# Every second pair of expert-up units by Strassen's seven block products, sums on GpSimd, all lowering on VectorE

## The reference, cut to what matters

```python
def peer(h, w_query, sub_keys1, sub_keys2, expert_down, expert_up):
    ...
    u = expert_down[ib]
    act = jax.nn.gelu(jnp.einsum("td,thkd->thk", hb, u), approximate=False)
    v = expert_up[ib]
    return jnp.einsum("thk,thkd->td", gb * act, v)
```

## Time and profile before

| | |
|---|---|
| median of 3 runs (lowest to highest) | 1389.7 us (1389.6 to 1393.01) |
| profiled execution, its own time | 1390.32 us |
| its span, first to last instruction | 1388.5 us |
| PE busy | 1362.2 us, 98% |
| DVE busy | 1037.2 us, 75% |
| ACT busy | 887.4 us, 64% |
| POOL busy | 653.5 us, 47% |

### The profile page before, as it was taken

The page is one execution under the profiler, slowest core; times in us unless marked ns, Lnnn a source line. Parts: engine busy times, 40 slices in busy tenths (PEclk is TensorE's granted clock), DMA queues, the critical chain, the costliest instruction groups (busy, mean ns, idle before and its releaser), DMA issues.

```text
span 1388.5 us, 32152 instructions
## 1 busy us (share of the span) xinstructions
PE 1362.2 (98%) x9840; PEld 1267.2 (91%) x9840; DVE 1037.2 (75%) x2233; ACT 887.4 (64%) x1861; POOL 653.5 (47%) x503
## 2 busy tenths in 40 slices
PE   7999999999999999999999999999999999999998
PEld 4798999999999989999999999999998888888886
DVE  6778867888988496439999868888876666666665
ACT  5668765555446665547888687777765555555554
POOL 4896783000006868688888887777730000000000
PEclk9999999999999999999999999999999999999998
DMA  9776565988983633565555554444455666566662
GB/s 343 272 253 228 198 244 189 323 320 317 336 331 122 215 127 123 188 216 168 182 182 183 182 168 154 159 156 151 154 166 194 195 192 189 194 196 193 189 194 90
DMA packets 79798, 283.84 MB, mean 204 GB/s; under 512 B 8822, under 2 KB 8950, under 8 KB 79611
## 3 DMA queue, kind: packets, MB, share of 16 engines
q1 hardware_dynamic: 79738, 283.07, 59.7%
HBM read 281.99 MB, written 1.05 MB: 204 GB/s over the span
## 4 chain that ended last, share of the span: by engine, by line
PE 79%; POOL 6%; issue 5%; PEld 3%; DVE 3%; ACT 2%; DMA 1%; PEldq 0%; POOLq 0%; SPq 0%; DVEq 0%
PE psA L1821 19%; PE psA L1825 19%; PE psA L1824 19%; POOL w_lo L563 6%; PE psD L1821 6%; PE psD L1824 5%; PE psD L1825 5%; PE psD L2283 1%; PEld psA L1821 1%; PE psD L2284 1%; PEld psA L1825 1%; PEld psA L1824 1%; DMA xT<-x 1%; DVE arena L1540 1%; PEld psD L2240 0%
## 5 line engine op out<-in xcount | busy, mean ns | idle before, releaser
L628 ACT CAST w_hi<-raw 128x512 fp32r<-128x512 f32 x864 | 529.5, 620 | 424.7 <-PE psA L1821 306.8
L563 POOL TENSOR_TENSOR w_lo<-raw,w_hi 128x512 fp32r<-128x512 f32 x476 | 632.7, 1348 | 353.6 <-ACT w_hi L628 343.1
L1821 PE MATMUL psA<-h_hi,w_hi 128*128 128x256 f32 x1568 | 452.8, 289 | 0.7 <-POOL w_lo L563 0.5
L1824 PE MATMUL psA<-h_lo,w_hi 128*128 128x256 f32 x1568 | 443.0, 283 | 0.0
L1825 PE MATMUL psA<-h_hi,w_lo 128*128 128x256 f32 x1568 | 442.9, 282 | 0.0
L1099 DVE TENSOR_TENSOR w_lo<-raw,w_hi 128x512 fp32r<-128x512 f32 x388 | 266.1, 691 | 152.7 <-ACT w_hi L628 151.6
L1821 PEld LDWEIGHTS psA<-h_hi,w_hi 128*128 128x128 f32 x1568 | 300.0, 191 | 4.3 <-issue 1.5
L1824 PEld LDWEIGHTS psA<-h_lo,w_hi 128*128 128x128 f32 x1568 | 300.2, 191 | 0.1
L1825 PEld LDWEIGHTS psA<-h_hi,w_lo 128*128 128x128 f32 x1568 | 299.9, 191 | 0.0
L1821 PE MATMUL psA<-w_hi,u_hi 128*128 128x512 f32 x512 | 199.4, 389 | 0.4 <-DVE u_lo L1162 0.4
L1825 PE MATMUL psA<-w_hi,u_lo 128*128 128x512 f32 x512 | 199.2, 389 | 0.0
(11 more groups left out here) (391 smaller groups left out, 2212.5 us busy)
## 6 DMA issues: line engine op xcount, KB each, us to landing
raw<-expert_down SPq DMA_DIRECT2D x128, 512.0 KB, 3.2
raw<-expert_up SPq DMA_DIRECT2D x128, 512.0 KB, 4.2
arena<-ada SPq DMA_DIRECT2D x96, 512.0 KB, 5.3
raw<-gateup SPq DMA_DIRECT2D x44, 512.0 KB, 5.4
raw<-feat SPq DMA_DIRECT2D x28, 512.0 KB, 3.8
raw<-win SPq DMA_DIRECT2D x24, 512.0 KB, 3.3
raw<-down SPq DMA_DIRECT2D x22, 512.0 KB, 6.1
raw<-wout SPq DMA_DIRECT2D x20, 512.0 KB, 3.2
```

Source lines behind the costliest of these rows:

```text
L563: nc.gpsimd.tensor_tensor(w_lo[:, s * HALF:(s + 1) * HALF], raw_half(n), w_hi[:, s * HALF:(s + 1) * HALF].bitcast(F32), ALU.subtract).then ...
L628: nc.scalar.copy(w_hi[:, n % SLOTS * HALF:(n % SLOTS + 1) * HALF], raw_half(n)).then_inc(hi_ready, 1)
L1821: first = mm(o, w[0], m[0], start=start, stop=False, skip_group_check=True)
L1824: mm(o, w[0], m[1], start=False, stop=False, skip_group_check=True)
```

## The change

The first 16 expert-up units and the last four stay as they were. The 108 between them become 27 groups of four: two units in the old way ("singles", 12 matmuls each) and one pair of units as a product of 2x2 blocks. Of a pair, U gives the blocks a11, a12, a21, a22 (unit by token block) and W gives b11, b12, b21, b22 (unit by half). Strassen's method, in Winograd's form, takes seven products instead of eight, 21 matmuls instead of 24, each of a block or a sum of blocks of U with a block or a sum of blocks of W (three blocks and four sums on either side):

- POOL makes four sums of 128x512 for W (`sum_weights`, into `w_sums`) and four of 128x128 for U (`sum_pairs`, one of them written over a21).
- ACT copies seven halves of W for a pair (three blocks, four sums), and the U blocks and sums as one 128x512 and one 128x384.
- DVE lowers all of them, as it did before: 11 halves in a group in place of eight, and the same two pieces of U.
- `w_hi` and `w_lo` get eight slots in place of four; every second pair from the fourth on is loaded into `raw_spare`.
- Four of the seven products add into the four banks of `psD`. After the last group ACT copies one bank, DVE adds the banks into `y_sums` (four adds), and the final copies of `psA` become adds of `psA` and `y_sums`, all on DVE.

The core of the diff:

```diff
+def up_lowered(g, i):
+    return UP_AT + GROUP_HALVES * g + i + 1
...
@@ SP
+            def load_singles(g):
+                for k in range(2):
+                    if g == 0:
+                        sp.wait_ge(lo_ready, UP_AT - 6 + 2 * k)
+                    else:
+                        single_free(g - 1, k)
...
@@ POOL
+            def sum_weights(g, k, in0, in1, op, read):
+                if g:
+                    pool.wait_ge(lo_ready, up_lowered(g - 1, read))
+                if k in (2, 3):
+                    pool.wait_ge(sem("w_sums"), 4 * g + (1, 3)[k - 2])
+                nc.gpsimd.tensor_tensor(w_sums[:, k, :], in0, in1, op).then_inc(sem("w_sums"), 1)
+            def sum_pairs(g):
+                c = PLAIN_UPS + 4 * g + 2
+                a11, a21, a12, a22 = [U[:, c + k // 2, k % 2 * P:(k % 2 + 1) * P] for k in range(4)]
+                if g:
+                    pool.wait_ge(sem("pair_lo"), 2 * g)
+                nc.gpsimd.tensor_tensor(u_sums[:, 0, :], a21, a22, ALU.add).then_inc(sem("u_sums"), 1)
...
+            sum_pairs(0)
+            for g in range(GROUPS_UP):
+                b11, b12, b21, b22 = [pair_raw(g, k // 2, k % 2) for k in range(4)]
+                pair_in(g)
+                sum_weights(g, 0, b12, b11, ALU.subtract, 5)
+                sum_weights(g, 1, b22, b12, ALU.subtract, 7)
+                sum_weights(g, 2, b22, w_sums[:, 0, :], ALU.subtract, 8)
+                sum_weights(g, 3, b21, w_sums[:, 2, :], ALU.subtract, 10)
+                if g + 1 < GROUPS_UP:
+                    sum_pairs(g + 1)
@@ ACT
-            for h in range(2):
-                act.wait_ge(sem("y_banks"), 2 * h + 1)
-                nc.scalar.copy(y_tok[:, 0, h * HALF:(h + 1) * HALF], psA[:, 2 * h, :]).then_inc(sem("y_first"), 1)
@@ DVE
+            def lower_up(n, src):
+                dve.wait_ge(hi_ready, n + 1)
+                hi, lo = up_half(n)
+                V.tensor_tensor(lo, src, hi.bitcast(F32), ALU.subtract).then_inc(lo_ready, 1)
...
+            for g in range(GROUPS_UP):
+                n = UP_AT + GROUP_HALVES * g
+                lower_up(n, single_raw(0, 0))
+                lower_up(n + 1, pair_raw(g, 0, 0))
+                lower_u(g + 1, 0)
...
+                lower_pair_sums(g + 1)
+                lower_up(n + 9, single_raw(1, 1))
+                lower_up(n + 10, w_sums[:, 3, :])
...
+            dve.wait_ge(sem("y_sums_0"), 1)
+            for dst, src, bank in ((1, 0, 2), (2, 1, 1), (1, 1, 3), (3, 2, 3)):
+                own(V.tensor_tensor(y_sums[:, dst, :], y_sums[:, src, :], psD[:, bank, :], ALU.add))
...
-                V.tensor_copy(y_tok[:, 1, h * HALF:(h + 1) * HALF], psA[:, 2 * h + 1, :]).then_inc(sem("y_second"), 1)
+                V.tensor_tensor(y_tok[:, 0, h * HALF:(h + 1) * HALF], psA[:, 2 * h, :], y_sums[:, 2 * h, :],
+                                ALU.add).then_inc(sem("y_first"), 1)
+                V.tensor_tensor(y_tok[:, 1, h * HALF:(h + 1) * HALF], psA[:, 2 * h + 1, :], y_sums[:, 2 * h + 1, :],
+                                ALU.add).then_inc(sem("y_second"), 1)
@@ PE
+            for g in range(GROUPS_UP):
+                single(g, 0, 0, 0)
+                mixed(g, 1, A11, psD[:, 0, :], start=g == 0)
+                mixed(g, 2, A12, psA[:, 0, :])
+                single(g, 3, 0, 1)
+                mixed(g, 4, S4, psA[:, 2, :])
+                mixed(g, 5, S1, psD[:, 1, :], start=g == 0)
+                single(g, 6, 1, 0)
+                mixed(g, 7, S3, psD[:, 3, :], start=g == 0)
+                done = mixed(g, 8, S2, psD[:, 2, :], start=g == 0)
...
+                single(g, 9, 1, 1)
+                mixed(g, 10, A22, psA[:, 1, :])
```

More of the change, by code:

```diff
@@ L75, with spare_pair, pair_before, pair_loads @@
 DVE_LOWERS = 128
+PLAIN_UPS = 16
+GROUPS_UP = (P - PLAIN_UPS - LAST_EXPERTS) // 4
+GROUP_HALVES = 11
+UP_SLOTS = 8
+FIRST_UP = UNITS - P + PLAIN_UPS
+UP_AT = 2 * FIRST_UP
+LAST_AT = UP_AT + GROUP_HALVES * GROUPS_UP
+def up_lowered(g, i):
+    return UP_AT + GROUP_HALVES * g + i + 1
+LAST_LOWERED = LAST_AT
+def spare_pair(g):
+    return g >= 3 and g % 2 == 1
+def pair_before(g):
+    return g - 1 if g < 3 else 2 if g == 4 else g - 2
+def pair_loads(g):
+    if spare_pair(g):
+        return (g - 1) // 2
+    return FIRST_UP // 4 + (g if g < 3 else 2 + (g - 2) // 2)
+LAST_PAIR_LOADS = pair_loads(GROUPS_UP - 1) + 1
 DVE_FIRST = 61
@@ L348, in two_mixers_program, with up_half, pair_raw, single_raw @@
         U = arena[:, :].rearrange("p (e t) -> p e t", t=T)
+        w_hi_more = at_place("w_hi_more", H_AT, 4 * HALF, F32R)
+        w_lo_more = at_place("w_lo_more", H_AT + 4 * HALF, 4 * HALF, F32R)
+        def up_half(n):
+            s = n % UP_SLOTS
+            at = s % SLOTS * HALF
+            hi, lo = (w_hi, w_lo) if s < SLOTS else (w_hi_more, w_lo_more)
+            return hi[:, at:at + HALF], lo[:, at:at + HALF]
+        PAIR = 7 * P
+        pair_parts = [[at_place(f"pair_{k}{g}", ARENA + (2 * g + z) * PAIR, PAIR, F32R)[:, :]
+                       for z, k in enumerate(("hi", "lo"))] for g in range(2)]
+        u_sums = part(arena, 4 * PAIR, 3, P)
+        assert 4 * PAIR + 3 * P <= PLAIN_UPS * T
+        raw_spare = part(arena, PLAIN_UPS * T, 2, 2 * HALF)
+        w_sums = part(late, 0, 4, HALF)
+        y_sums = part(late, 0, 4, HALF)
+        def pair_raw(g, k, h):
+            src = raw_spare[:, k, :] if spare_pair(g) else raw[:, (2 + k) * 2 * HALF:(3 + k) * 2 * HALF]
+            return src[:, h * HALF:(h + 1) * HALF]
+        def single_raw(k, h):
+            return raw[:, (2 * k + h) * HALF:(2 * k + h + 1) * HALF]
         def row(i):
@@ L527, in _, with pair_free @@
             stream(lambda u: expert_down[u], 128)
-            stream(lambda u: expert_up[:, u, :], 128 - LAST_EXPERTS)
-            for h in range(2):
-                for u in range(128 - LAST_EXPERTS, 128, 2):
-                    load(expert_up[:, u:u + 2, h * HALF:(h + 1) * HALF], HALF)
+            stream(lambda u: expert_up[:, u, :], PLAIN_UPS)
+            def pair_free(g, k):
+                sp.wait_ge(lo_ready, up_lowered(g, (1, 4)[k]))
+                sp.wait_ge(sem("w_sums"), 4 * g + (2, 4)[k])
@@ new lines, in load_singles @@
+            def load_singles(g):
+                for k in range(2):
+                    if g == 0:
+                        sp.wait_ge(lo_ready, UP_AT - 6 + 2 * k)
+                    else:
+                        single_free(g - 1, k)
+                    sp.dma_start(raw[:, k * 1024:(k + 1) * 1024],
+                                 expert_up[:, PLAIN_UPS + 4 * g + k, :]).then_inc(raw_full[k], 16)
+            load_singles(0)
+            load_pair(0)
+            for g in range(1, GROUPS_UP):
+                load_pair(g)
+                load_singles(g)
@@ new lines, in _ @@
+            for h in range(2):
+                for k in range(2):
+                    if h == 0:
+                        single_free(GROUPS_UP - 1, k)
+                    else:
+                        pair_free(GROUPS_UP - 1, k)
+                    u = 128 - LAST_EXPERTS + 2 * k
+                    dst = raw[:, (2 * h + k) * 1024:(2 * h + k + 1) * 1024].rearrange("p (a n) -> p a n", n=HALF)
+                    sp.dma_start(dst, expert_up[:, u:u + 2, h * HALF:(h + 1) * HALF]).then_inc(
+                        raw_full[2 * h + k], 16)
@@ L1044, in final_square @@
+            act.wait_ge(sem("p_banks"), 1)
+            act.wait_ge(lo_ready, LAST_LOWERED)
+            nc.scalar.copy(y_sums[:, 0, :], psD[:, 0, :]).then_inc(sem("y_sums_0"), 1)
+            for k in range(4, 8):
+                upper_last(k)
             def final_square(j, n):
@@ L2312, in _, with single, mixed @@
                 expert(j, j + 1, first=j == 0)
-            with repeat(pe, P // 4 - 2, {halves: 8}) as i:
+            with repeat(pe, PLAIN_UPS // 4 - 1, {halves: 8}) as i:
                 for j in range(4):
                     expert(j, i * 4 + (j + 5))
+            def single(g, i, k, h):
+                pe.wait_ge(sem("u_lo"), PLAIN_UPS + 2 * g + k + 1)
+                pe.wait_ge(lo_ready, up_lowered(g, i))
+                w = up_half(halves.n)
+                halves.n += 1
+                slot = g % 2 * 2 + k
+                for t in range(NT):
+                    u = [part_[:, slot, t * P:(t + 1) * P] for part_ in (u_hi, u_lo)]
+                    product(psA[:, 2 * h + t, :], u, w, start=False, stop=False, opens=t == 0)
+            A11, S3, A12, A22, S1, S2, S4 = range(7)
+            def mixed(g, i, u_at, o, start=False):
+                pe.wait_ge(sem("pair_lo"), 2 * g + (1 if u_at <= A22 else 2))
+                pe.wait_ge(lo_ready, up_lowered(g, i))
+                w = up_half(halves.n)
+                halves.n += 1
+                u = [part_[:, u_at * P:(u_at + 1) * P] for part_ in pair_parts[g % 2]]
+                return product(o, u, w, start=start, stop=False, opens=True)
+            pe.wait_ge(sem("gated"), T // GROUP)
```

(8 more changed lines are left out.)

146 lines of the change are left out of this document (127 added, 19 removed).

## The result

The changed kernel takes 1472.98 us in the median of four runs (1471.53 to 1474.79), the kernel before 1389.88 in the same session: a ratio of 1.0593, interval 1.0574 to 1.0612. The forecast was 1473.

What follows compares the result with a forecast made beforehand. DVE, slowed by POOL's sums, was to replace PE as the bound: groups +81.3, last group -2.8, end +4.3, together +82.8 us on the profiled 1390.3, so 1473 us; range 1450 to 1505, 8 in 10.

Steps and rivals of the forecast that it cites:

- What bounds: In the groups, DVE becomes the bound, busy almost without a break; PE waits for `lo_ready`, some 3.7 us per group.
- The deciding term: In the groups, POOL's sums hold up DVE, 1.09 us per large, 0.27 per small: 13.89 us per group, +81.3 in all.
- Durations add: Rival, 3 in 100: in the groups each engine waits for the other's whole instruction; 16.66 us per group, 1547 us.
- DVE's durations and POOL's: In the groups, DVE's mean 128x512 lowering rises from 692 to about 1000 ns, POOL's sums from 1.29 to about 1.8 us.
- Start: From the last plain half to the first group: 5.1 us of preparation fit PE's 5.2 us of matmuls, costing nothing.
- Last group: The last of the 27 groups prepares no next U, which saves DVE work: -2.8 us.
- Loads: Loads of singles and pairs in the groups, 4.2 us each to land: cost nothing, but would show if DVE did not slow down.
- End: After the groups: last four units take PE 14.5 us for 10.88, +3.7; the two last adds of `psA` +0.6; together +4.3.
- Sum: Whole kernel: 81.3 - 2.8 + 4.3 = +82.8 us on the profiled 1390.3, so 1473 us.
- The clock: A sign to check in the groups: PE's granted clock should be 1.00.
- The engines do not meet: Rival, 4 in 100: in the groups sums and lowerings don't clash, PE stays the bound at 10.20 us; 1375 us.
- The clock falls: Rival, 2 in 100: PE, waiting in pieces, drops to 1.2 GHz; a group takes 20.4 us, +257, about 1650 us.

Runs made afterwards that it cites:

- the second run: The changed kernel with only the four 128x128 sums of U replaced by POOL memsets, the four large sums kept: 1446.62 us, ratio 1.0394.
- The first run: The changed kernel with all eight sums of a group replaced by POOL memsets, which write but read nothing, semaphores kept: 1376.49 us, ratio 0.9891.
- the third: The changed kernel with all eight sums made by DVE itself between its lowerings, POOL idle: 1416.45 us, ratio 1.0178.
- the later runs: The changed kernel with Strassen in 18 of 27 groups, sums on DVE: 1388.93 us; and in 14 of 27, sums on POOL: 1390.49 us.

## Why the prediction was right

**What bounds.** Right: DVE busy for 40 of 40 us, PE waiting for `lo_ready`. PE's waits are pieces of up to 1.4 us; they add up to 50.5 us in 1120:1430, 2.2 per group, but by the distances between starts PE lost 13.80 - 10.20 = 3.6 per group, where 3.7 was forecast. The rest lies in matmuls that ran at the lower clock or are shown as longer than the distance to the next.

**The deciding term.** 13.89 us per group, measured 13.80. Both prices were right: 1.09 for a large sum is what the single instructions show (1.09 to 1.11), and 0.27 for a small one, which had no row, came out at 0.25 to 0.26 in the timeline and 0.26 by the second run. The first run shows that POOL's reading causes it and not its writing, the third that it is the pairing of engines and not the work.

**Durations add.** Wrong, as weighed: by this rival the period would have been 16.66, and it is 13.80. The Trainium skill ("SBUF — State Buffer", section "Who interferes with whom") is right here on who contends; that whoever comes second is blocked for the other's whole instruction does not fit the 13.80. (12 x 0.69 + 2 x 0.42 + 0.56 is 9.68 and not 9.70; this changes nothing.)

**DVE's durations and POOL's.** The mean of a 128x512 lowering was put at about 1000 ns and came out between 0.95 and 1.2 us for most groups of rows; POOL's large sum at about 1.8 and came out at 1.6.

**Start.** Priced at nothing. The first three groups took 17.07, 11.16 and 16.42 us, 44.65 for three, or 3.3 over three steady ones. Counted in the timeline, 15 large sums ran in them and not 12; three sums of the fourth group had come early, and 3 x 1.09 = 3.3. (Of these 3.3, 0.55 us is shown as a wait of DVE at 1099; a sum on POOL fell into it and cost the next lowering only 0.47.)

**Last group.** Priced at -2.8, so 11.1 us; it took 7.8. It is the same three sums: only one large sum (at 1433.03) was left for it, and DVE alone needs 8.45 - 1.74 = 6.71, with 1.09 more 7.80. A sum costs its 1.09 in whichever group it falls, so over 27 groups both terms together were right: 369.7 us of lowerings, 372.2 by my terms.

**Loads.** Priced at nothing, and nearly so: DVE's only wait in the groups is that one, for ACT, which waited for a load. That loads would show if DVE did not slow down came true in the later runs, with 5.9 and 6.9 us.

**End.** Its steps came in the order forecast, but later, and one was left out. From the last lowering of the groups, which ends at 1440.67, the tail on DVE:

```profile
1445.57 0.69 DVE L1986 TENSOR_TENSOR w_lo<-raw,w_hi 128x512 fp32r<-128x512 f32 x1
...
1447.12 2.84 DVE L2041 TENSOR_TENSOR late<-late,psD 128x512 f32<-128x512 f32 x4
1450.10 1.90 DVE L1986 TENSOR_TENSOR w_lo_more<-raw,w_hi_more 128x512 fp32r<-128x512 f32 x3
...
1457.80 0.69 DVE L2048 TENSOR_TENSOR arena<-psA,late 128x512 f32<-128x512 f32 x1 [1.53 <-PE psA L2098]
1458.41 0.68 DVE L2050 TENSOR_TENSOR arena<-psA,late 128x512 f32<-128x512 f32 x1
```

Half 2 was ready 5.6 us after the groups (4.9 by my working), the four adds took 2.84 (2.8), half 4 was ready at 10.1 (9.1), and the two last adds do follow each other, 0.61 apart. Then PE's last four halves took 6.8 us and not 4 x 1.36: eight transposes stand among them (a distance of 1.29 us between matmuls, at 1453.5), and my working left them out. The kernel before has them too, with 1.02 us, so its last four units took 11.8 and not 10.88. From the end of the groups' lowerings PE needed 16.9 us, 5.2 more than before, where 14.5 and 3.7 were forecast.

**Sum.** The profiled execution grew by 82.3; 82.8 was forecast. The groups gave 2.5 less than their terms, the last four units 1.5 more, the two last adds their 0.6, and PE began the stage 0.4 us later than before, ahead of the change. So part of the closeness of 1473 is luck: misses of opposite sign cancel.

**The clock.** The one sign that was wrong: 1.00 was expected throughout. It is told in the last section, since it cost nothing.

**The rivals.** *The engines do not meet* failed on its premise, and the first run shows the time that it would have given. *The clock falls* had its premise for a part of the time, without its price.

## What to carry to other kernels

A helper engine is not free because it is idle: GpSimd's sum, which reads SBUF, cost VectorE with its two SBUF inputs 1.09 us, and 0.60 is what VectorE needs to make that sum itself. Price such an offload from a stretch of the old trace where both engines are full, by distances between starts, and ask whether the helped engine has that much slack in each period. And a saving on the engine that sets the pace (here 0.68 us a group) is worth what the next engine leaves of it, so spread it: with VectorE making the sums, sixteen such groups with plain ones between them gained 8.6 us where twenty-seven in a row lost 25.

## What the runs showed of the hardware that was not expected

**The granted clock.** It was 0.91 in the window from 1140 to 1180, above, and 1.00 from 1260 to 1300, in the same rhythm of work. The PE timeline shows it within a group:

```profile
1197.98 0.76 PE L2094 MATMUL psA<-w_hi,u_hi 128*128 128x512 f32 x1 [1.22 <-DVE w_lo L1986]
...
1199.40 0.63 PE L2094 MATMUL psA<-w_hi,u_hi 128*128 128x512 f32 x1
1199.83 0.63 PE L2097 MATMUL psA<-w_lo,u_hi 128*128 128x512 f32 x1
...
1204.34 0.40 PE L2094 MATMUL psD<-w_hi_more,pair_hi 128*128 128x512 f32 x1
```

After two waits of 1.36 and 1.22 us, with three matmuls between them, matmuls start 0.43 us apart, at the lower of the two levels (1.2 GHz), and from 1204.3 on 0.23 apart, at 2.4. The group still takes 13.83, since DVE sets the pace. What tells the stretches with this from those without isn't settled.

**Who is held.** In the steady groups of the change each POOL sum held one DVE instruction; in the second run POOL was at times the one held, by several DVE instructions in a row. The sums that were held cost DVE no less later, 1.10 each.

**Reading alone counts.** POOL wrote the same tiles in the first run, in 528 ns for 128x512, and DVE's lowerings beside it kept to 690 ns (692 before).
